# Two edits to a two-layer decoder kernel: steps moved in the first mixer's input projection and at the stage boundaries, and the down projections' input placed 256 bytes further in SBUF

## What is computed

```python
for layer in range(DEPTH):
    y = rmsnorm(h, norm_g[layer, 0])
    y = even_mixer(y, ...) if layer % 2 == 0 else odd_mixer(y, ...)
    h = h + rmsnorm(y, norm_g[layer, 1])
    y = conv_ffn(rmsnorm(h, norm_g[layer, 2]), ...)
    h = h + rmsnorm(y, norm_g[layer, 3])
```

## Time and profile before

| | |
|---|---|
| three timed runs | 697.79, 701.14, 701.19 us; median 701.14 |
| profiled execution | 698.03 us, with a span of 696.2 us from first to last instruction |
| TensorE | 673.5 us busy, 97% of the span |
| VectorE / ScalarE / GpSimd | 434.9 / 358.9 / 155.6 us busy |
| mean granted TensorE clock | 0.999 |
| DMA | 116.21 MB, mean 167 GB/s |

### The profile page before, as it was taken

One profiled execution on the slowest core, in us unless ns is written; L12 is line 12 of the kernel. 1 busy time (PEld: TensorE's weight loads), 2 busy tenths in 40 slices (PEclk: granted clock), 3 DMA queues, 4 the chain that ended last, 5 costly groups with the idle time before them and its releaser, 6 DMA issues.

```text
span 696.2 us, 11381 instructions
## 1 busy us (share of the span) xinstructions
PE 673.5 (97%) x4357; PEld 595.0 (85%) x4359; DVE 434.9 (62%) x580; ACT 358.9 (52%) x499; POOL 155.6 (22%) x117
## 2 busy tenths in 40 slices
PE   4989999999999999999999999999999999999996
PEld 3878887778799999998887999777789999998885
DVE  4587775577775757576436654576675757575532
ACT  5555425476475555656334634375475656566320
POOL 0022220000113434343001000372113434343000
PEclk9999999999999999999999999999999999999999
DMA  8947643001355354545653746301445363634601
GB/s 336 395 154 280 226 176 120 1 2 61 121 199 225 139 223 146 215 153 180 271 186 117 249 175 233 130 1 62 181 159 233 129 234 124 237 126 182 237 0 60
DMA packets 18652, 116.21 MB, mean 167 GB/s; under 512 B 2463, under 2 KB 3133, under 8 KB 5693
## 3 DMA queue, kind: packets, MB, share of 16 engines
q1 hardware_dynamic: 17325, 111.52, 43.0%
q10 hardware_dynamic: 1296, 4.26, 1.8%
HBM read 114.72 MB, written 1.05 MB: 166 GB/s over the span
## 4 chain that ended last, share of the span: by engine, by line
PE 88%; issue 4%; DVE 3%; ACT 3%; POOL 2%; DMA 1%; DVEq 0%; POOLq 0%; ACTq 0%
PE ps L1134 24%; PE ps L1136 23%; PE ps L1135 23%; PE ps L1176 3%; PE ps L1324 2%; PE ps L1250 1%; PE ps L1284 1%; PE ps L1528 1%; POOL rstd L1049 1%; PE ps L1129 1%; PE ps L1517 1%; PE ps L1260 1%; DVE xn L644 1%; PE ps L1410 1%; ACT whi L329 1%
## 5 line engine op out<-in xcount | busy, mean ns | idle before, releaser
L615 DVE TENSOR_TENSOR wlo<-raw,whi 128x2048 fp32r<-128x2048 f32 x99 | 227.0, 2322 | 73.3 <-ACT whi L329 73.3
L329 ACT CAST whi<-raw 128x2048 fp32r<-128x2048 f32 x99 | 186.1, 1917 | 72.3 <-PE ps L1136 67.9
L1134 PE MATMUL ps<-xhi,whi 128*128 128x256 f32 x768 | 217.9, 284 | 0.0
L1135 PE MATMUL ps<-xlo,whi 128*128 128x256 f32 x768 | 217.7, 284 | 0.0
L1136 PE MATMUL ps<-xhi,wlo 128*128 128x256 f32 x768 | 217.7, 283 | 0.0
L1134 PEld LDWEIGHTS ps<-xhi,whi 128*128 128x128 f32 x768 | 147.6, 192 | 0.0
L1135 PEld LDWEIGHTS ps<-xlo,whi 128*128 128x128 f32 x768 | 147.6, 192 | 0.0
L1136 PEld LDWEIGHTS ps<-xhi,wlo 128*128 128x128 f32 x768 | 147.6, 192 | 0.0
L513 ACT ACTIVATE conv<-ps,c_conv 128x256 f32<-128x256 f32 x88 | 42.5, 563 | 101.7 <-PE ps L1136 100.2
L1089 POOL TENSOR_TENSOR hidf<-act_g,conv 128x512 f32<-128x512 f32 x22 | 74.1, 3369 | 83.6 <-ACT act_g L519 83.6
L947 DVE SCALAR_TENSOR_TENSOR conv<-ps,c_conv,conv 128x255 f32<-128x255 f32 x88 | 38.4, 478 | 77.4 <-ACT conv L513 76.9
(11 more groups left out here) (172 smaller groups left out, 811.4 us busy)
## 6 DMA issues: line engine op xcount, KB each, us to landing
raw<-in_weights SPq DMA_DIRECT2D x101, 1024.0 KB, 4.9
c_gpre<-in_gpre ACTq DMA_DIRECT2D x4, 512.0 KB, 4.8
raw<-in_weights SPq DMA_DIRECT2D x4, 512.0 KB, 8.3
c_gpost<-in_gpost ACTq DMA_DIRECT2D x4, 512.0 KB, 5.0
h<-in_x SPq DMA_DIRECT2D x2, 512.0 KB, 7.7
out<-h SPq DMA_DIRECT2D x4, 256.0 KB, 2.0
t<-in_masks SPq DMA_DIRECT2D x1, 512.0 KB, 14.4
c_rope<-in_rope SPq DMA_DIRECT2D x1, 256.0 KB, 14.2
```

Of the source, the lines that this page charges most:

```text
L329: act.copy(whi[:, slot, :], raw[:, slot, :]).then_inc(hi_done, 1)
L615: dve.tensor_tensor(wlo[:, slot, :], raw[:, slot, :], whi[:, slot, :].bitcast(F32), ALU.subtract).then_inc(lo_done, 1)
L1134: pe.matmul(out, s_hi, m_hi, start=start, stop=False, skip_group_check=shared)
L1135: pe.matmul(out, s_hi, m_lo, start=False, stop=False, skip_group_check=shared)
```

## The change

It moves steps and adds one tensor; nothing is computed differently.

1. `("turn", 1)` stands behind `("unit", 2, 1)`, no longer ahead of it. `rotate(1)` moves on VectorE from the step `("unit", 1, 1)` to `("unit", 2, 0)`. The split of `xb_parts` (ScalarE's cast, VectorE's subtraction) moves from `x2T` to `("unit", 1, 1)`, behind that step's weight unit.
2. In `junction(p)` for p = 0, 1, 2 both low parts of token tile 0 stand behind the residual of tile 1; before, they stood ahead of it.
3. In `first_units` the products with `xlo` of unit u0 stand behind all products with `xhi` of both units. The two units are released together at the end.
4. `hid_shift`, 256 bytes a partition and never read or written, is declared ahead of `hid_hi`. `hid_hi`, `hid_lo`, `conv`, `act_g` and `hidf` so lie 256 bytes further: `hid_hi` is now 166 x 512 + 384 bytes behind `whi`.

```diff
+        sb("hid_shift", [P, SEQ // 4], F32, a)
         hid_hi = sb("hid_hi", [P, FT, SEQ], F32R, a)
...
-                      ("unit", 2, 0), ("cmp1", 0, 0), ("turn", 1), ("unit", 2, 1), ("cmp1", 0, 1),
+                      ("unit", 2, 0), ("cmp1", 0, 0), ("unit", 2, 1), ("turn", 1), ("cmp1", 0, 1),
...
+                elif step == ("unit", 1, 1):
+
                     act.wait_ge(xb_sum, 4)
                     act.wait_ge(xb_pad, 1)
...
                 post_ms_of(p, 1)
-                if Y_ORDER[p] is HALF_MAJOR:
-                    post_gain(p, 1, 1)
-                if p < 3:
-                    pre_los(p + 1, 0, (0,))
-                if Y_ORDER[p] is TILE_MAJOR:
-                    post_gain(p, 1, 1)
-                if p < 3:
-                    pre_los(p + 1, 0, (1,))
+                post_gain(p, 1, 1)
                 post_residual(p, 1)
                 if p < 3:
+                    pre_los(p + 1, 0)
                     pre_ms_of(p + 1, 1)
                     pre_normed(p + 1, 1)
                     pre_los(p + 1, 1)
...
-                elif step[0] == "unit" and step[2] == 1 and 1 <= step[1] <= 5:
-                    if step[1] == 1:
-                        dve.wait_ge(tables_in, 16 * TABLES)
-                        dve.wait_ge(mask_cast, 1)
+                elif step[0] == "unit" and step[2] == 1 and 2 <= step[1] <= 5:
                     rotate(step[1])
+                elif step == ("unit", 2, 0):
+
+                    dve.wait_ge(tables_in, 16 * TABLES)
+                    dve.wait_ge(mask_cast, 1)
+                    rotate(1)
...
                 for t in range(TT):
-                    for i in range(2):
-                        u = u0 + i
-                        pe.wait_ge(pre_hi, 2 * (p * TT + t) + i + 1)
+                    for u in (u0, u0 + 1):
...
-                            products(xhi, whi, u, range(4), t)
+                            high(u, range(4), t)
                             products(xhi, wlo, u, range(4), t)
-                        if t == 0 and i == 1:
-                            pre(p, 1)
-                        pe.wait_ge(pre_lo, 2 * (p * TT + t) + i + 1)
-                        ins = products(xlo, whi, u, range(4), t)
-                        if t == TT - 1:
-                            ins.then_inc(unit_used, 1)
-                    if t == 0 and tile_ready is not None:
+                    low(u0, t)
+                    if t == 0:
+                        pre(p, 1)
+                    ins = low(u0 + 1, t)
+                    if t == TT - 1:
+                        ins.then_inc(unit_used, 2)
+                    elif tile_ready is not None:
                         ins.then_inc(tile_ready, 1)
```

More of the change, by code:

```diff
@@ L645, in pre_normed, with pre_los @@
                                              c_gpre[:, colhalf(c)], ALU.mult, ALU.mult).then_inc(pre_xn, 1)
-            def pre_los(p, t, halves=range(2)):
+            def pre_los(p, t):
                 tok = slice(t * P, (t + 1) * P)
-                for c in halves:
+                for c in range(2):
                     dve.wait_ge(pre_hi, 2 * (p * TT + t) + c + 1)
@@ L746, in _ @@
                                       wg_parts[:, :, 0:NSA_HEADS * BRANCH].bitcast(F32), ALU.subtract).then_inc(wg_done, 1)
-                elif step[0] == "unit" and step[2] == 1 and 1 <= step[1] <= 5:
-                    if step[1] == 1:
-                        dve.wait_ge(tables_in, 16 * TABLES)
-                        dve.wait_ge(mask_cast, 1)
+                elif step[0] == "unit" and step[2] == 1 and 2 <= step[1] <= 5:
                     rotate(step[1])
+                elif step == ("unit", 2, 0):
+                    dve.wait_ge(tables_in, 16 * TABLES)
+                    dve.wait_ge(mask_cast, 1)
+                    rotate(1)
+                elif step == ("unit", 1, 1):
+                    dve.wait_ge(xb_hid, 1)
+                    dve.tensor_tensor(xb_parts[:, :, :, CPAD:CPAD + 2 * NC], xbf[:].rearrange("p a (k n) -> p a k n", k=CKT),
+                                      xb_parts[:, :, :, 0:2 * NC].bitcast(F32), ALU.subtract).then_inc(xb_split, 1)
                 elif step == ("gateT",):
@@ L766, in _ @@
                             ins.then_inc(xb_sum, 1)
-                    dve.wait_ge(xb_hid, 1)
-                    dve.tensor_tensor(xb_parts[:, :, :, CPAD:CPAD + 2 * NC], xbf[:].rearrange("p a (k n) -> p a k n", k=CKT),
-                                      xb_parts[:, :, :, 0:2 * NC].bitcast(F32), ALU.subtract).then_inc(xb_split, 1)
                 elif step == ("hidT",):
@@ L1179, in products, with high, low @@
                     return ins
+                def high(u, blocks, t):
+                    pe.wait_ge(pre_hi, 2 * (p * TT + t) + u - u0 + 1)
+                    return products(xhi, whi, u, blocks, t)
+                def low(u, t):
+                    pe.wait_ge(pre_lo, 2 * (p * TT + t) + u - u0 + 1)
+                    return products(xlo, whi, u, range(4), t)
                 for t in range(TT):
-                    for i in range(2):
-                        u = u0 + i
-                        pe.wait_ge(pre_hi, 2 * (p * TT + t) + i + 1)
+                    for u in (u0, u0 + 1):
                         if p == 0 and t == 0:
                             pe.wait_ge(first_hi, u + 1)
-                            products(xhi, whi, u, (0, 1), t)
+                            high(u, (0, 1), t)
                             pe.wait_ge(first_lo, u + 1)
@@ L1190, in first_units @@
                             pe.wait_ge(hi_done, u + 1)
-                            products(xhi, whi, u, (2, 3), t)
+                            high(u, (2, 3), t)
                             pe.wait_ge(lo_done, u + 1)
```

## The result

| | before | after |
|---|---|---|
| runs | 697.79 to 701.19, median 698.83 (6) | 693.35 to 694.91, median 693.53 (6) |
| profiled execution / span | 698.03 / 696.2 us | 694.86 / 693.1 us |
| mean granted clock | 0.999 | 0.995 |

The ratio is 0.9926 (0.9905 to 0.9948): 5.3 us between the medians, where 7.0 were forecast from a median of 701.14.

What follows compares the result with a forecast made beforehand. TensorE, busy 97% of the span at full clock, was taken as the bound, so only its idle time or matmul pace could gain. 2.2 + 1.9 + 2.9 = 7.0 us, 701.14 - 7.0 = 694.1 us; range 690.0 to 698.0.

Steps and rivals of the forecast that it cites:

- Part 1: First mixer's turn: TensorE's wait for GpSimd's sum goes, 2.2 us gained, between 0 and 2.3.
- The slack: First mixer: GpSimd's adds end near 50.1, 2.8 us before TensorE asks for the sum.
- Part 2: Boundaries 0, 1 and 2: residual ahead of low parts gains 0.7 + 0.6 + 0.6 = 1.9 us, between 1.1 and 2.4.
- the second source: Boundaries 1 and 2: eight transposes take 1.32 us against 1.09 in the mixer's turn, the last four waiting for the second half.
- Part 3: `first_units`: low parts' first reader moves behind eight more matmuls (1.8 us); costs nothing itself and makes part 2 free.
- Part 4: Down projections: shifting `hid_hi` brings 528 matmuls to the output projection's pace, 2.9 us gained; worst end 10.3 us lost.
- the gate row: Gate's matmuls, `wg_parts` at +384 from `xhi`: 117 ns for 256 columns against 120.1 in the up projection, so no penalty.
- The prediction's own sign for the first rival: Down projections: a pace of 232 ns would show that the address doesn't set the pace.
- The first rival: Down projections: pace doesn't depend on the address; 4.1 us remain, 697.0 us; chance 0.22.
- The turn's wait: Input projection: the wait moves but doesn't go, TensorE stops at 53 or soon behind; 4.8 us gained, 696.3; chance 0.08.
- the worse position: Down projections: the new address is slower than the old, up to 10.3 us lost, 707.3 us; chance 0.05.
- the prediction's last sign: Whole kernel: the prediction is wrong if the span falls by less than 3.5 us.

Runs made afterwards that it cites:

- regroup_only: Kernel before with only the regrouped products of `first_units`, VectorE's old order kept: 699.61 us, ratio 0.9996.
- los_late: Kernel before with only VectorE's low parts of tile 0 moved behind the residual, TensorE's old order kept: 697.28 us, ratio 0.9968.
- w_shift: Changed kernel with 128 bytes of padding ahead of `whi` and 128 instead of 256 ahead of `hid_hi`: 691.81 us, ratio 0.9882.
- shift_only: Kernel before with only the 256 bytes ahead of `hid_hi`: 699.49 us, ratio 0.9997.
- boundary_only: Kernel before with only the boundaries' later low parts and the regrouped `first_units`: 697.35 us, ratio 0.9965.
- shift384: Changed kernel with 384 bytes instead of 256 ahead of `hid_hi`: 690.79 us, ratio 0.9873.
- shift128: Changed kernel with 128 bytes instead of 256 ahead of `hid_hi`: 690.63 us, ratio 0.9872.
- shift64: Changed kernel with 64 bytes instead of 256 ahead of `hid_hi`: 691.56 us, ratio 0.9886.
- shift192: Changed kernel with 192 bytes instead of 256 ahead of `hid_hi`: 694.14 us, ratio 0.9933.

## Why the prediction held, and where it was wrong

- **Part 1, 2.2 us: right.** Measured 2.26 in the trace and 2.3 alone. The reckoning of VectorE's order was right within 0.6 us at each step (rotation at 43.62 against 44.1, next unit at 46.15 against 46.6), and GpSimd's sum at 49.64 against 50.1. The slack was 3.0 us against 2.8.
- **Part 2, 0.7 + 0.6 + 0.6 = 1.9 us: right.** Measured 0.74 + 0.65 + 0.74 = 2.1 in the trace, 1.9 alone. Of the idle time of 0.90, 0.37 and 0.37 us ahead of the transposes under 0.1 us is left, and at boundaries 1 and 2 these take 1.12 and 1.03 us in place of 1.32, the second source that the reckoning had named.
- **Part 3, nothing by itself and what makes part 2 free: right**, by `regroup_only` (0) and `los_late` (1.0 us less). I had not priced what part 2 would lose without it; it is half.
- **Part 4, 2.9 us: wrong, 0.** The idea that the pace depends on the operands' distance was right, and so was the size: 226.8 ns is to be had, for 3.0 us, with 128 or 384 bytes. What failed is the step "I take the gain of 2.9 us, since the gate row is nearest in position". I had written positions modulo 512, with no row that showed 512 to be the period; modulo 256 the change goes from 128 to 128, a move to the same place. The gate's row was no evidence. It doesn't even stand for +384 alone: from one contraction step to the next `wg_parts` advances 256 bytes and `xhi` 1,024, so every second of its matmuls stood at +128, the position that the shift was to leave. And its matmuls have 256 columns and half as wide a load: `w_shift` shows that the up projections' 256-column matmuls pay nothing at 128, and the gate's 2 ns. The prediction's own sign for the first rival, a down pace of 232 ns, is what came.
- **The first rival** (the pace doesn't depend on the address) had nearly the right gain, 4.1 us against 4.4, for a wrong reason; its time, 697.0, missed by 3.5 us, because it started from the same 701.14. The Trainium skill's two independent SBUF read ports (TensorE: Matmul & The Clock Gate, "Step-by-step: what each phase is for") would make all six rows of the table alike. They go from 226.8 to 233.3 ns, and the measurement decides.
- **The turn's wait** did not come back, and the worse position did not come: the rivals of 696.3 and 707.3 us are out. A position worse than the old one does exist, 64 past a multiple of 256, at 0.9 ns and 0.5 us.
- **The time, 694.1 against 693.53, is right by luck.** Of the 7.0 us, 4.4 came, or 5.3 between medians. But 701.14 was the median of three runs, two of them at the upper level; six runs give 698.83, and 693.53 lies at the lower level of after. A start 2.3 us too high and a gain 1.7 us too large cancel to 0.6. By the prediction's last sign, a span that falls by less than 3.5 us, the two profiled executions, 3.1 us apart, speak against it as a whole; the fall of the clock in after's holds 1.5 of that, and the lowest runs are 4.4 apart. The range has slips as well: its own terms, 0.1 + 0.5 at the bottom and 0.8 at the top, give 690.2 to 697.8 and not 690.0 to 698.0. "I know of nothing in the change that picks a level" was wrong as well: see the clock, below.

## What to carry to other kernels

When two matmul stages of the same shape run at different paces, compare the distance of stationary and streaming operand modulo 256 bytes in SBUF: padding one buffer so that it is 0 gave 5.6 ns a matmul (2.4%) for one line, and a pad that doesn't change that residue gives nothing. This was measured for float32r, 512 streaming columns and 128-column loads; matmuls of 256 columns in the up projections showed no such price. Before a pad is chosen, try two or three sizes; one row at another shape doesn't tell the period. When a producer is moved behind the path's own work, move its first reader as well: the half of the boundary change on VectorE kept only half of its gain without the regrouped matmuls. When timed runs stand at levels, price a change against one level.

## What the runs showed that I had not expected

**The distance modulo 256.** Six positions, four paces: 226.8 ns at 0, 228.9 at 192, 232.4 at 128, 233.3 at 64, for float32r matmuls of 512 columns with 128-column loads. What in the chip does this isn't shown.

**The clock falls behind short waits, in some runs.** In the profiles of `shift_only`, `boundary_only`, `regroup_only` and `los_late` the turn's wait of 2 us is followed by 3.4 us at 1.2 GHz. Windows of `shift_only`:

```profile
46.00:50.00 4.00, 1.95 (x17) 1.69 (x16) 4.00 (x2) 0.00 (x0) 3.35 (x2) 1.00 0.69 209
50.00:54.00 4.00, 4.00 (x15) 3.23 (x14) 1.97 (x2) 3.31 (x3) 0.00 (x0) 0.57 0.81 311
54.00:58.00 4.00, 4.00 (x22) 3.34 (x21) 2.21 (x2) 1.65 (x2) 0.00 (x0) 1.00 0.64 221
```

TensorE was busy half of the first window, at full clock, and all of the second, at 0.57. These four profiled executions took 699.46, 697.39, 699.58 and 698.63 us, each 1.4 to 2.0 above its kernel's lowest run; the profile of before (698.03) has no such fall. In `after` and `w_shift` it comes behind the wait for `sb_a`; behind the same wait of 1.4 us the profiles of `shift384`, `shift128`, `shift64` and `shift192` have none. So a wait of 2.0 us costs 2.0, or 3.5 when the clock falls behind it, and removing the turn's wait removed one of the two places for a fall: part 1 alone took five of its six runs to one level, which makes its gain 3.9 us between medians where it is 2.3 between lowest runs. The third level of before, 701.2, would be a fall at both places; no profile caught one, so that is argued only.
